# First norm's root multiplied in behind the u tiles' products, and three products of zeros on TensorE ahead of the first weights

## The chip, the cores and the metric

The kernel runs on one core of one Trainium2 chip. The core has five engines that run their own instruction streams and meet only at semaphores: TensorE (PE, matrix products into PSUM banks), VectorE (DVE), ScalarE (ACT), GpSimd (POOL) and SyncE (SP, which issues all of this kernel's transfers). The metric is device time in microseconds (us), as the median of several executions.

## The reference

A recurrent and attention block, and then two further blocks with their own mixers and feed-forwards, on 512 tokens of width 1024. Only its beginning matters here: the first norm, the projection to u and the convolution over u.

```python
D_MODEL = 1024
SEQ = 512
CONV_WIDTH = 4
def rms_norm(x, g):
    xf = x.astype(jnp.float32)
    y = xf * lax.rsqrt(jnp.mean(xf * xf, axis=-1, keepdims=True) + NORM_EPS)
    return (y * g.astype(jnp.float32)).astype(x.dtype)
...
        h = rms_norm(x, norm_g[l])
        proj = jnp.einsum("bsd,de->bse", h, w_in[l])
        u = proj[..., OFF_RNN_X:OFF_RNN_G]
...
        q = proj[..., OFF_Q:OFF_K].reshape(B, S, N_Q_HEADS, HEAD_DIM)
...
        u = causal_depthwise_conv(u, conv_w[l], conv_b[l])
        y_rnn = rg_lru(u, lru_w_a[l], lru_b_a[l], lru_w_x[l], lru_b_x[l], lru_lambda[l]) * jax.nn.silu(g_rnn)
```

The root is one number per token. The projection mixes features and not tokens, so the root can be multiplied in before the product or behind it; the gain g is one number per feature and must come before.

## The kernel before

Activations lie transposed: features on the 128 partitions in 8 chunks of 512 tokens each (`X`, `H_hi`, `H_lo`; `ch(t, k)` is chunk k). Every weight matrix is cut into tiles of 128 output features by 1024 input features, and the 269 tiles come in one stream in a fixed order: tiles 0 to 7 give u, 8 to 15 the queries (`T_Q` = 8), and so on. Products of 32-bit numbers are made as three faster ones: ACT rounds each half of a weight tile to `W_hi` (`split_hi`), DVE makes the rest `W_lo` (`split_lo`), and the activations are split in the same way, so that a tile costs 24 products of 128x512 (`linear`): W_hi by H_hi, W_hi by H_lo, W_lo by H_hi for each of 8 chunks. Tiles 0 and 1 are done together, chunk by chunk (`linear_pair`), because their chunks arrive one at a time from the norm.

The order of all work is written out by hand, engine by engine, with semaphores between. The start goes so: SP issues the parameters, four pairs of chunks of X, weight tile 0, the constants, weight tiles 1 to 3 and more, all in one queue. ACT squares the chunks, DVE adds the squares to `SS`, PE sums them over partitions (`square_sums`), DVE and ACT make the root (`variance`, `root`, `inverse`), PE spreads it over the partitions of a bank (`stat_rows`), and then DVE makes each chunk of X times gain times root (`norm_lo`, L1503), ACT its rounded part `H_hi` (L941), DVE its rest `H_lo` (L1495), and PE the pair.

Behind the pair, PE goes through tiles 2 to 7. After each it does the gates of a u tile that is ready (`gates(i)`, two products of 32-bit numbers). Meanwhile DVE goes through the u tiles in `U_ORDER` (L1543 to L1562): a step i waits for the tile's products, makes the convolution from the bank (one scaling, L1552, and three shifted multiply-adds, L1555, each waiting for the one before), frees the bank, then does one step of the later blocks' modulation (`ada_at`, L1447, from tile 2 on) and the rests of a coming weight tile (`split_lo(Tile(i + 1))`, for i above 2). PE starts tile t only when `lo_done` shows its W_lo. A short chain of 128x8 operations for the recurrence's constants (L1520 to L1531) stands on DVE ahead of the sums of squares. POOL writes zeros into three buffers at the start and later multiplies I by U (L1360).

Of the kernel before, what the change touches and what calls it, by code (L numbers as in the profile page):

```python
# [15 lines left out]
P = 128  # L16
S = 512
# [190 lines left out]
def build(nc, x, stream, ada, crow, lru_w, prm, cst, rope1, pos, out):  # L208
    with ExitStack() as ctx:
# [109 lines left out]
        stat_mm, t1_done, h_hi_done, h_lo_done = sem("stat_mm"), sem("t1_done"), sem("h_hi_done"), sem("h_lo_done")  # L319
        x_final = sem("x_final")  # L320
        u_done, gate_mm, gate_out = sem("u_done"), sem("gate_mm"), sem("gate_out")
        b2_done, root_b = sem("b2_done"), sem("root_b")
# [31 lines left out]
        def ch(t, j, n=S):  # L354
            return t[:, ds(j * S, n)]


        SPN = COL[:, 0:8]
# [26 lines left out]
        def _(sp):  # L385
# [14 lines left out]
            for k in range(4):  # L400
                sp.dma_start(X[:, 2 * k * S:2 * (k + 1) * S], x[:, 2 * k * S:2 * (k + 1) * S]).then_inc(x_in[k], 16)
            raw(Tile(0), False)
# [61 lines left out]
        def _(pe):  # L464
            def linear(tile, hi, lo, chunks=KC, first=None, between=None, own=True):

                dst = ps[tile.bank][:]
                free = tile.uses if own else tile.uses - 1
                if not (isinstance(free, int) and free == 0):
                    pe.wait_ge(bank_free[tile.bank], free)  # L470
                for half in range(2):
                    sl = (2 * tile.slot + half) % 4
                    pe.wait_ge(lo_done, tile.n * 2 + (half + 1))
                    ks = range(4 * half, min(4 * half + 4, chunks))
                    for k in ks:
# [4 lines left out]
                        pe.matmul(dst, wh, ch(hi, k), start=(k == 0), stop=False)  # L480
                        pe.matmul(dst, wh, ch(lo, k), start=False, stop=False)  # L481
                        mm = pe.matmul(dst, wl, ch(hi, k), start=False, stop=(k == chunks - 1))  # L482
# [28 lines left out]
            def linear_pair(t0, idx, bank=PAIR_BANK):  # L511
# [5 lines left out]
                for k in range(KC):  # L517
# [11 lines left out]
                    mm = pe.matmul(ps[b.bank][:], W_hi[:, at[1]:at[1] + P], ch(H_lo, k), start=False, stop=(k == 7))  # L529
                mm.then_inc(used, 2)  # L530

            def square_sums(z, parts, last, need=None):
# [119 lines left out]
            linear(Tile(T_Q), H_hi, H_lo, between=lambda k: gates(6 + k // 4) if k in (1, 5) else None)  # L652
            for c in range(1, 10):
# [257 lines left out]
        def _(act):  # L911
# [23 lines left out]
            def norm_hi(idx, shift=None, third=None):  # L935
                for k in range(KC):
                    if k == 7 and third is not None:
                        split_hi(third, (0,), ACT.Identity)
                    act.wait_ge(t1_done, 8 * idx + k + 1)
# [20 lines left out]
            act.activation(COL[:, 88:96], COL[:, 80:88], ACT.Exp).then_inc(prm_done, 1)  # L960
            for k in range(KC):
                if k % 2 == 0:
                    act.wait_ge(x_in[k // 2], 16)
                square(k, k)
            split_hi(Tile(0))
            split_hi(Tile(1))
# [8 lines left out]

            split_hi(Tile(2), (1,))
            act.wait_ge(crow_in, 16)
# [373 lines left out]
        def _(pool):  # L1351
# [67 lines left out]
        def _(dve):  # L1419
# [96 lines left out]
            dve.tensor_tensor(COL[:, 80:88], COL[:, 72:80], lam, ALU.min).then_inc(prm_done, 1)  # L1516

            dve.wait_ge(prm_done, 2)
            e = COL[:, 88:96]
# [12 lines left out]

            for k in range(KC - 2):
                sum_square(k, k == 0)
            dve.wait_ge(sq_done, 8)
            dve.tensor_tensor(ch(SQ, 1), ch(SQ, 0), ch(SQ, 1), ALU.add).then_inc(ss_step, 1)
            split_lo(Tile(0))
            split_lo(Tile(1))
            inv_rms(0)
            norm_lo(0, lambda k: pr("norm_g", k), None, Tile(2))  # L1540
            split_lo(Tile(2), (1,))

            for i, t in enumerate(U_ORDER):  # L1543
# [726 lines left out]
def STAT_ROWS(z):  # L2270

    return 2 * z + 2
# [88 lines left out]
```

## Time and profile before

| what | us |
|---|---|
| three runs | 1737.07, 1738.52, 1734.59; median 1737.07 |
| span of the profiled execution | 1734.7 |
| PE busy in it | 1668.1 (96%) |
| DVE, ACT, POOL busy | 1015.6 (59%), 703.0 (41%), 76.8 (4%) |
| first product of the pair begins | 19.23 |
| first product behind the pair (tile 2) begins | 31.97 |

The span runs from the first instruction of the core to its last; the profiled execution is one of its own, and no separate device time is shown for it beside the span. A busy share is a mean over 1.7 ms of stages; the change touches the first 80 us, and these are read from the rows by time.

### The profile page before, as it was taken

The page shows a single profiled execution, that of the slowest core. Times are in us where ns is not written, and L with a number is a line of the kernel's source. Part 1 is how long each engine was busy: PE and PEld are TensorE (multiplying, and loading weights), DVE is VectorE, ACT ScalarE, POOL GpSimd, SP SyncE. Part 2 cuts the span into 40 slices and gives each one's busy share as a digit, 9 for nine tenths or more (in the row PEclk, how much of TensorE's full clock was granted, in tenths as well). Part 3 has the DMA queues.
Part 4 walks back from the last instruction along what each step waited for, and adds up shares of the span by engine and source line. Part 5 has one row for each costly group of instructions (what it writes and reads, how often), then busy time and mean ns, then how long its engine had stood idle before and what let it go on. Part 6 is the DMA issues. An engine that isn't in the chain of part 4 may idle for free.

```text
span 1734.7 us, 23016 instructions
## 1 busy us (share of the span) xinstructions
PE 1668.1 (96%) x7756; PEld 1329.5 (77%) x7756; DVE 1015.6 (59%) x2004; ACT 703.0 (41%) x1329; POOL 76.8 (4%) x61
## 2 busy tenths in 40 slices
PE   6999999999999998888999999999999899999999
PEld 5777777778877775467888888887888788888887
DVE  7788876665467797835655563466454533333334
ACT  5364676653343335753333323234223433332322
POOL 0020000000000073100000000000000000000000
PEclk9999999999999998999999999999999999999999
DMA  6453444444331120002455553352333233333333
GB/s 241 158 158 113 146 153 154 156 149 137 97 97 49 49 86 25 1 25 73 170 193 194 193 195 121 121 182 86 97 97 97 73 98 97 97 97 97 97 97 110
DMA packets 56775, 202.82 MB, mean 117 GB/s; under 512 B 6576, under 2 KB 6704, under 8 KB 56560
## 3 DMA queue, kind: packets, MB, share of 16 engines
q1 hardware_dynamic: 56688, 201.68, 35.5%
q8 instruction: 52, 0.85, 0.2%
q14 instruction: 35, 0.29, 0.1%
HBM read 198.38 MB, written 2.10 MB: 116 GB/s over the span
## 4 chain that ended last, share of the span: by engine, by line
PE 88%; DVE 6%; ACT 2%; issue 2%; DMA 1%; SPq 0%; POOL 0%; DVEq 0%; ACTq 0%; POOLq 0%
PE bank L480 25%; PE bank L482 25%; PE bank L481 25%; PE bank L584 2%; PE bank L639 2%; PE bank L618 1%; PE bank L523 1%; PE bank L524 1%; DVE W_lo L1433 1%; PE bank L538 1%; DVE SB L2042 1%; DVE AW L1447 1%; PE bank L725 1%; PE bank L744 1%; PE bank L526 1%
## 5 line engine op out<-in xcount | busy, mean ns | idle before, releaser
L480 PE MATMUL bank<-H_hi,W_hi 128*128 128x512 f32 x1336 | 534.5, 400 | 3.3 <-DVE W_lo L1433 2.2
L481 PE MATMUL bank<-H_lo,W_hi 128*128 128x512 f32 x1336 | 521.7, 390 | 0.0
L482 PE MATMUL bank<-H_hi,W_lo 128*128 128x512 f32 x1336 | 521.6, 390 | 0.0
L1433 DVE TENSOR_TENSOR W_lo<-RAW,W_hi 128x512 fp32r<-128x512 f32 x538 | 351.4, 692 | 180.6 <-ACT W_hi L919 164.4
L919 ACT ACTIVATE W_hi<-RAW 128x512 fp32r<-128x512 f32 x538 | 317.3, 625 | 271.6 <-PE bank L482 235.3
L480 PEld LDWEIGHTS bank<-H_hi,W_hi 128*128 128x128 f32 x1336 | 251.3, 188 | 73.4 <-issue 19.7
L481 PEld LDWEIGHTS bank<-H_lo,W_hi 128*128 128x128 f32 x1336 | 251.6, 188 | 54.4 <-issue 4.5
L482 PEld LDWEIGHTS bank<-H_hi,W_lo 128*128 128x128 f32 x1336 | 251.4, 188 | 53.2
L482 PE MATMUL bank<-A_hi,W_lo 128*128 128x512 f32 x352 | 137.1, 390 | 0.0
L481 PE MATMUL bank<-A_lo,W_hi 128*128 128x512 f32 x352 | 137.1, 390 | 0.0
L480 PE MATMUL bank<-A_hi,W_hi 128*128 128x512 f32 x352 | 137.1, 389 | 0.0
L1447 DVE CUSTOM_DVE_ANT_0 AW<-AW,CROW 128x1024 f32<-128x1024 f32 x96 | 118.0, 1230 | 8.3 <-DVE X L2150 3.7
L1159 ACT ACTIVATE G<-bank 128x512 f32<-128x512 f32 x60 | 35.9, 598 | 170.3 <-PE bank L482 170.3
L956 ACT CAST A_hi<-Y 128x512 f32 (+1 forms) x44 | 27.3, 620 | 185.0 <-DVE Y L2122 185.0
L2122 DVE TENSOR_TENSOR Y<-bank,G 128x512 f32<-128x512 f32 x44 | 30.4, 692 | 118.0 <-PE bank L482 116.6
L480 PEld LDWEIGHTS bank<-A_hi,W_hi 128*128 128x128 f32 x352 | 66.1, 188 | 13.7
L482 PEld LDWEIGHTS bank<-A_hi,W_lo 128*128 128x128 f32 x352 | 66.1, 188 | 13.7
L481 PEld LDWEIGHTS bank<-A_lo,W_hi 128*128 128x128 f32 x352 | 66.1, 188 | 13.6
L2150 DVE SCALAR_TENSOR_TENSOR X<-bank,MOD,X 128x512 f32 x32 | 24.0, 751 | 75.9 <-PE bank L482 75.8
L2127 DVE TENSOR_TENSOR A_lo<-Y,A_hi 128x512 f32 (+1 forms) x44 | 30.5, 692 | 42.5 <-ACT A_hi L956 42.5
L584 PE MATMUL bank<-KD,Q 64*128 64x256 f32 (+3 forms) x256 | 45.8, 438 | 7.0 <-DVE SM L2042 3.1
L480 PE MATMUL bank<-YA_hi,W_hi 128*128 128x512 f32 x128 | 50.0, 391 | 1.6 <-DVE YA_lo L2084 1.6
(263 smaller groups left out, 2007.8 us busy)
## 6 DMA issues: line engine op xcount, KB each, us to landing
RAW<-weights SPq DMA_DIRECT2D x269, 512.0 KB, 3.7
AW<-ada SPq DMA_DIRECT2D x100, 512.0 KB, 3.7
X<-x_t SPq DMA_DIRECT2D x4, 512.0 KB, 5.5
y_t<-X SPq DMA_DIRECT2D x8, 256.0 KB, 2.0
LW<-lru_w SPq DMA_DIRECT2D x1, 1024.0 KB, 12.6
QX<-QR SPq DMA_DIRECT2D x40, 16.0 KB
CROW<-crow SPq DMA_DIRECT2D x1, 512.0 KB, 10.7
ROPE<-rope SPq DMA_DIRECT2D x1, 512.0 KB, 13.4
```

The lines of the kernel that those rows point to most:

```text
L480: pe.matmul(dst, wh, ch(hi, k), start=(k == 0), stop=False)
L481: pe.matmul(dst, wh, ch(lo, k), start=False, stop=False)
L482: mm = pe.matmul(dst, wl, ch(hi, k), start=False, stop=(k == chunks - 1))
L584: mm = pe.matmul(dst, Q[rows, chunk * S + n * P:chunk * S + (n + 1) * P], KD[rows, k0:k0 + w], start=True, stop=True)
L639: mm = pe.matmul(ps[6][odd * HD:(odd + 1) * HD, 0:2 * P], V[:, at_col:at_col + HD], PT[:, c * S + odd * 2 * P:c * S + (odd + 1) * 2 * P], ...
L919: act.activation(W_hi[:, sl * HALF:(sl + 1) * HALF], RAW[:, c:c + HALF], fn).then_inc(hi_done, 1)
L956: act.copy(dst, ch(Y2, par)).then_inc(a_hi_done, 1)
L1159: act.activation(ch(G1, par), ps[PAIR_BANK if first else ga.bank][:], fn).then_inc(fn_done, 1)
L1433: dve.tensor_tensor(W_lo[:, w], RAW[:, c:c + HALF], W_hi[:, w], ALU.subtract).then_inc(lo_done, 1)
L1447: dve.tensor_tensor_reduce(out=w, in0=w, in1=CROW[:], scale=1.0, scalar=0.0, op0=ALU.mult, op1=ALU.add, accum_out=MODQ[:, q:q + 1]).then_i ...
L2122: dve.tensor_tensor(ch(Y2, par), ps[tile.bank][:], ch(G1, par), ALU.mult).then_inc(prod_done, 1)
L2127: dve.tensor_tensor(ch(A_lo[g % 2], jj), ch(Y2, par), ch(A_hi[g % 2], jj), ALU.subtract).then_inc(a_lo_done, 1)
```

## The change

PE no longer waits for the root. The u tiles are made from X times gain (`XG_hi` from ACT, `XG_lo` from DVE), and DVE multiplies each u tile by the root when it takes it from the bank, into `G1`, from where the convolution now reads. The sums of squares go to PE between chunks 5 and 7 of the pair (`first_pair`), the spreading of the root into tile 2 (`first_rows`), and ACT copies it to `ROOT`. The true normed chunks are still needed from tile 8 on: POOL makes X times root (`XR`), and ACT and DVE split it (`x_true`) during tiles 2 to 6, by the table `TRUE_AT`. Two weight tiles are moved ahead of the last three pairs of X on SP, the chain of 128x8 operations moves behind the rests of tile 2 on DVE, and PE gets three products of zeros before the pair.

```diff
+        def xg_hi(k):
+            return ch(XG_hi, k)
...
+                if k == 0:
+                    raw(Tile(0), False)
+                    raw(Tile(1), False)
             sp.dma_start(CS[:], cst).then_inc(consts_in, 16)
-            for n in range(1, 4):
+            for n in range(2, 4):
...
+            def first_pair(a, b):
+
+                for k in range(KC):
+                    if k % 4 == 0:
+                        pe.wait_ge(lo_done, b.n * 2 + k // 4 + 1)
+                    pe.wait_ge(xg_hi_done, k + 1)
...
+                    pe.wait_ge(xg_lo_done, k + 1)
...
+                    if k == 5:
+                        pe.wait_ge(consts_in, 16)
+                        square_sums(0, (SS,), False, (ss_step, 6))
+                        square_sums(0, (ch(SQ, 1),), True, (ss_step, 7))
...
-            pe.wait_ge(consts_in, 16)
-            square_sums(0, (SS,), False, (ss_step, 6))
-            norm_stat(0, (ss_step, 7))
-            linear_pair(T_U, 0, 5)
+            def first_rows(k):
+                if k == 1:
+                    pe.wait_ge(rinv_done, 1)
+                    stat_rows(16, 2).then_inc(stat_mm, 1)
+
+            pe.wait_ge(pool_chain, 3)
+            for n in range(3):
+                pe.matmul(ps[3][:], QX1[0][:, 0:P], QX1[1][:, :], start=True, stop=True)
+            first_pair(Tile(T_U), Tile(T_U + 1))
             for t in range(T_U + 2, T_Q):
-                linear(Tile(t), H_hi, H_lo, own=t > 2)
+                linear(Tile(t), xg_hi, xg_lo, own=t > 2, between=first_rows if t == 2 else None)
                 gates(t - 2)
...
+            act.wait_ge(prm_in, 16)
+            for pair in range(4):
+                act.wait_ge(x_in[pair], 16)
+                x_gained(2 * pair)
+                x_gained(2 * pair + 1)
+                if pair == 0:
+                    split_hi(Tile(0))
+                    split_hi(Tile(1))
+                else:
+                    square(2 * pair - 2, 2 * pair - 2)
+                    square(2 * pair - 1, 2 * pair - 1)
...
             for t in range(T_U + 2, T_Q):
                 split_hi(Tile(t + 1))
+                for k in TRUE_AT[t]:
+                    x_true(k)
                 gates_out(t - 2)
...
+            pool.wait_ge(root_row, 1)
+            for k in range(KC):
+                pool.wait_ge(x_in[k // 2], 16)
+                if k >= 2:
+                    pool.wait_ge(h_lo_done, k - 1)
+                pool.tensor_tensor(ch(XR, k % 2), ch(X, k), ROOT[:, 0:S], ALU.mult).then_inc(xr_done, 1)
...
+            def x_true(k):
+                dve.wait_ge(h_hi_done, k + 1)
+                dve.scalar_tensor_tensor(out=ch(H_lo, k), in0=ch(XR, k % 2), scalar=pr("norm_g", k), in1=ch(H_hi, k),
+                                         op0=ALU.mult, op1=ALU.subtract).then_inc(h_lo_done, 1)
...
-                src = ps[5] if t == 0 else ps[tile.bank]
-
-                link(dve.tensor_scalar(ch(U, t), src[:], pr("conv_w", 24 + t), pr("conv_b", t), ALU.mult, ALU.add))
+                if i == 0:
+                    dve.wait_ge(root_row, 1)
+                src = ch(G1, i % 2)
+                link(dve.tensor_tensor(src, (ps[5] if t == 0 else ps[tile.bank])[:], ROOT[:, 0:S], ALU.mult))
+                dve.sem_inc(bank_free[tile.bank], 1)
+
+                link(dve.tensor_scalar(ch(U, t), src, pr("conv_w", 24 + t), pr("conv_b", t), ALU.mult, ALU.add))
...
                 dve.wait_ge(u_done, i + 1)
-                dve.sem_inc(bank_free[tile.bank], 1)
+                for k in TRUE_AT.get(i, ()):
+                    x_true(k)
                 ada_at(t)
...
+TRUE_AT = {2: (0, 1), 3: (2, 3), 4: (4,), 5: (5, 6), 6: (7,), 7: ()}
```

The order on the engines at the places that the prediction speaks of follows. First PE at the start of the program, before: the sums of squares (L538), the spread root (L545), then the pair (L523 on).

```order
L538 MATMUL bank4<-CS_88,SS_106 128x1 [waits ss_step,consts_in]
L538 MATMUL bank4<-CS_88,SS_106 128x1 x3
L538 MATMUL bank4<-CS_88,SQ_102 128x1 [waits ss_step]
L538 MATMUL bank4<-CS_88,SQ_102 128x1 x3
L545 MATMUL bank2<-CS_88,VC_109 128x128 [waits rinv_done]
```

And the same place in the changed kernel: the products of zeros (L690), then the pair's first chunk.

```order
L690 MATMUL bank<-QX_116,QX_115 128x512 [waits pool_chain]
L690 MATMUL bank<-QX_116,QX_115 128x512 x2
L556 MATMUL bank<-XG_hi,W_hi 128x512 [waits xg_hi_done,lo_done]
L557 MATMUL bank<-XG_hi,W_lo 128x512
L556 MATMUL bank<-XG_hi,W_hi 128x512
L557 MATMUL bank<-XG_hi,W_lo 128x512
L559 MATMUL bank<-XG_lo_122,W_hi 128x512 [waits xg_lo_done]
```

Nothing that waits for the root stands in front of the pair any more. Second, DVE in step i = 2 of the u tiles and up to step 3, before:

```order
L1552 TENSOR_SCALAR U<-bank,PR 128x512 [waits u_done,used]
L1555 SCALAR_TENSOR_TENSOR U<-bank,PR,U 128x511 [waits dve_chain]
L1555 SCALAR_TENSOR_TENSOR U<-bank,PR,U 128x510 [waits dve_chain]
L1555 SCALAR_TENSOR_TENSOR U<-bank,PR,U 128x509 [waits dve_chain]
L1447 ISA AW,MODQ<-AW,CROW 128x1024 [waits u_done,crow_done,ada_in0]
```

and the same step in the changed kernel (V is the memory that `ROOT` takes, G_113 is `G1`):

```order
L1637 TENSOR_TENSOR G_113<-bank,V 128x512 [waits used,u_done]
L1640 TENSOR_SCALAR U<-G_113,PR 128x512 [waits dve_chain]
L1643 SCALAR_TENSOR_TENSOR U<-G_113,PR,U 128x511 [waits dve_chain]
L1643 SCALAR_TENSOR_TENSOR U<-G_113,PR,U 128x510 [waits dve_chain]
L1643 SCALAR_TENSOR_TENSOR U<-G_113,PR,U 128x509 [waits dve_chain]
L1593 SCALAR_TENSOR_TENSOR H_lo<-XR,PR,H_hi 128x512 [waits h_hi_done,u_done]
L1593 SCALAR_TENSOR_TENSOR H_lo<-XR,PR,H_hi 128x512 [waits h_hi_done]
L1515 ISA AW,MODQ<-AW,CROW 128x1024 [waits crow_done,ada_in0]
L1515 ISA MODQ 128x1
L1501 TENSOR_TENSOR W_lo<-RAW,W_hi 128x512 [waits hi_done] x2
```

The step has one instruction more in front, two rests of true chunks behind the convolution, and its shifted multiply-adds read two SBUF buffers where they read a bank and one buffer. Third, POOL in the changed kernel, behind its zeros; of these rows only the last was there before.

```order
L1424 TENSOR_TENSOR XR<-X,V 128x512 [waits x_in0,root_row,pool_chain]
L1424 TENSOR_TENSOR XR<-X,V 128x512 [waits x_in0]
L1424 TENSOR_TENSOR XR<-X,V 128x512 [waits h_lo_done,x_in1] x2
L1424 TENSOR_TENSOR XR<-X,V 128x512 [waits h_lo_done,x_in2] x2
L1424 TENSOR_TENSOR XR<-X,V 128x512 [waits h_lo_done,x_in3] x2
L1428 TENSOR_TENSOR I<-I,U 128x512 [waits u_done,gate_out] x8
```

Eight products of two SBUF buffers now run on POOL during the u tiles; from the third on each waits for a rest that DVE has made.

## Rows read from the trace of the kernel before

**Rows 1.** The page, parts 1 and 4: busy time, and the chain by engine.

```profile
PE 1668.1 (96%) x7756; PEld 1329.5 (77%) x7756; DVE 1015.6 (59%) x2004; ACT 703.0 (41%) x1329; POOL 76.8 (4%) x61
PE 88%; DVE 6%; ACT 2%; issue 2%; DMA 1%; SPq 0%; POOL 0%; DVEq 0%; ACTq 0%; POOLq 0%
```

**Rows 2.** Timeline 0 to 40 us: start, duration, instruction, idle time before it.

```profile
3.41 0.17 DVE L1520 TENSOR_SCALAR COL<-COL 128x8 f32<-128x8 f32 x1 [0.27 <-ACT COL L960]
...
5.34 1.15 ACT L928 ACTIVATE SQ<-X 128x512 f32<-128x512 f32 x2 [1.96 <-DMA X<-x_t]
...
6.55 0.17 DVE L1531 TENSOR_SCALAR COL<-COL 128x8 f32<-128x8 f32 x1
...
11.54 1.87 PE L538 MATMUL bank<-CS,SS 128*128 128x1 f32 x8 [11.54 <-DMA CS<-constants]
...
19.23 0.77 PE L523 MATMUL bank<-H_hi,W_hi 128*128 128x512 f32 x1 [1.58 <-ACT H_hi L941]
...
21.50 0.63 PE L529 MATMUL bank<-H_lo,W_hi 128*128 128x512 f32 x1
...
21.93 0.63 PE L523 MATMUL bank<-H_hi,W_hi 128*128 128x512 f32 x1
...
28.34 0.39 PE L523 MATMUL bank<-H_hi,W_hi 128*128 128x512 f32 x1
...
28.57 0.39 PE L524 MATMUL bank<-H_hi,W_lo 128*128 128x512 f32 x1
...
31.97 0.39 PE L480 MATMUL bank<-H_hi,W_hi 128*128 128x512 f32 x1
```

**Rows 3.** The page, part 6: transfers, size, time from issue to landing.

```profile
CROW<-crow SPq DMA_DIRECT2D x1, 512.0 KB, 10.7
ROPE<-rope SPq DMA_DIRECT2D x1, 512.0 KB, 13.4
```

**Rows 4.** Timeline of SP 0 to 140 us: the issues of these two.

```profile
5.87 0.58 SPq L406 DMA_DIRECT2D CROW<-crow  x1
...
6.97 0.49 SPq L408 DMA_DIRECT2D ROPE<-rope  x1
```

**Rows 5.** Timeline of DVE in the u tiles.

```profile
33.27 0.81 DVE L1552 TENSOR_SCALAR U<-bank,PR 128x512 f32<-128x512 f32 x1
...
59.46 0.81 DVE L1552 TENSOR_SCALAR U<-bank,PR 128x512 f32<-128x512 f32 x1 [1.07 <-PE bank L482]
...
66.66 0.81 DVE L1552 TENSOR_SCALAR U<-bank,PR 128x512 f32<-128x512 f32 x1 [1.22 <-PE bank L482]
...
71.24 1.29 DVE L1433 TENSOR_TENSOR W_lo<-RAW,W_hi 128x512 fp32r<-128x512 f32 x2
```

**Rows 6.** Timeline of PE at the start of tile 8 (after gates 5).

```profile
75.62 0.40 PE L481 MATMUL bank<-H_lo,W_hi 128*128 128x512 f32 x1
...
76.97 0.30 PEld L564 LDWEIGHTS bank<-U,LW 128*128 128x128 f32 x2 [0.46 <-issue]
```

**Rows 7.** Timeline of POOL.

```profile
84.86 12.37 POOL L1360 TENSOR_TENSOR I<-I,U 128x512 f32<-128x512 f32 x8 [82.65 <-ACT I L974]
```

**Rows 8.** Timeline of DVE, beside POOL's products and behind them.

```profile
92.08 1.78 DVE L1567 SCALAR_TENSOR_TENSOR T<-G,T 128x512 f32<-128x512 f32 x1
...
100.53 0.69 DVE L1567 SCALAR_TENSOR_TENSOR T<-G,T 128x512 f32<-128x512 f32 x1 [0.15 <-DVE Q L1586]
```

**Rows 9.** DVE's groups by line and form: busy, mean ns of one, idle before.

```profile
L2122 DVE TENSOR_TENSOR Y<-bank,G 128x512 f32<-128x512 f32 x44 | 30.4, 692 | 118.0 <-PE bank L482 116.6 <-ACT G L1159 1.3
...
L1497 DVE SCALAR_TENSOR_TENSOR H_lo<-G,MOD,H_hi 128x512 fp32r<-128x512 f32 x32 | 23.9, 748 | 1.0
```

**Rows 10.** Line 2196, a scaling from SBUF to SBUF: ns min/median/max.

```profile
L2196 DVE TENSOR_SCALAR ZC<-Y,PR x8: 481/486/488, 1202.5 to 1276.7; 128x512 f32 x6, 128x512 f32<-128x512 f32 x2
```

**Rows 11.** Busy time by stretch, with PE's granted clock (the number before the DMA share).

```profile
520.00:530.00 10.00, 7.51 (x25) 6.04 (x26) 7.90 (x16) 3.76 (x6) 0.00 (x0) 0.59 0.00 1
```

More of the change, by code:

```diff
@@ L256, in build @@
         W_lo = at("W_lo", 4 * HALF, dt=F32R)
+        kd = cursor[0]
         KD = at("KD", NKV * S)
@@ L355, in ch, with xg_lo @@
             return t[:, ds(j * S, n)]
+        def xg_hi(k):
+            return ch(XG_hi, k)
+        def xg_lo(k):
+            return ch(XG_lo[0], k) if k < 4 else ch(XG_lo[k // 2 - 1], k % 2)
         SPN = COL[:, 0:8]
@@ L479, in linear @@
                         wh, wl = W_hi[:, c:c + P], W_lo[:, c:c + P]
-                        pe.matmul(dst, wh, ch(hi, k), start=(k == 0), stop=False)
-                        pe.matmul(dst, wh, ch(lo, k), start=False, stop=False)
-                        mm = pe.matmul(dst, wl, ch(hi, k), start=False, stop=(k == chunks - 1))
+                        hk, lk = (hi(k), lo(k)) if callable(hi) else (ch(hi, k), ch(lo, k))
+                        pe.matmul(dst, wh, hk, start=(k == 0), stop=False)
+                        pe.matmul(dst, wh, lk, start=False, stop=False)
+                        mm = pe.matmul(dst, wl, hk, start=False, stop=(k == chunks - 1))
                         if k == ks[-1]:
@@ L530, in linear_pair @@
                 mm.then_inc(used, 2)
+            def first_pair(a, b):
[3 more added lines that the diff above has]
+                    pe.wait_ge(xg_hi_done, k + 1)
+                    at = [((2 * tile.slot + k // 4) % 4) * HALF + (k % 4) * P for tile in (a, b)]
+                    for dst, c in zip((ps[5], ps[b.bank]), at):
+                        pe.matmul(dst[:], W_hi[:, c:c + P], xg_hi(k), start=(k == 0), stop=False)
+                        pe.matmul(dst[:], W_lo[:, c:c + P], xg_hi(k), start=False, stop=False)
+                    pe.wait_ge(xg_lo_done, k + 1)
+                    mm = pe.matmul(ps[5][:], W_hi[:, at[0]:at[0] + P], xg_lo(k), start=False, stop=(k == 7))
+                    if k % 4 == 3:
+                        mm.then_inc(used, 1)
+                    mm = pe.matmul(ps[b.bank][:], W_hi[:, at[1]:at[1] + P], xg_lo(k), start=False, stop=(k == 7))
+                    if k == 7:
+                        mm.then_inc(used, 2)
+                    if k == 5:
+                        pe.wait_ge(consts_in, 16)
+                        square_sums(0, (SS,), False, (ss_step, 6))
+                        square_sums(0, (ch(SQ, 1),), True, (ss_step, 7))
             def square_sums(z, parts, last, need=None):
@@ L960, in _, with x_gained @@
             act.activation(COL[:, 88:96], COL[:, 80:88], ACT.Exp).then_inc(prm_done, 1)
[L961 to L966, printed above, removed]
+            def x_gained(k):
+                act.activation(xg_hi(k), ch(X, k), ACT.Identity, scale=pr("norm_g", k)).then_inc(xg_hi_done, 1)
+            def x_true(k):
+                act.wait_ge(xr_done, k + 1)
+                act.activation(ch(H_hi, k), ch(XR, k % 2), ACT.Identity, scale=pr("norm_g", k)).then_inc(h_hi_done, 1)
+            act.wait_ge(prm_in, 16)
[9 more added lines that the diff above has]
+                    square(2 * pair - 1, 2 * pair - 1)
+            square(6, 6)
+            square(7, 7)
             root(0, 1)
-            norm_hi(0, None, Tile(2))
+            split_hi(Tile(2), (0,))
             def gates_out(i):
@@ L976, in _ @@
             split_hi(Tile(2), (1,))
+            act.wait_ge(stat_mm, STAT_ROWS(0))
+            act.copy(ROOT[:, 0:S], ps[2][:]).then_inc(root_row, 1)
             act.wait_ge(crow_in, 16)
@@ L1516, in _, with x_rest, x_true @@
             dve.tensor_tensor(COL[:, 80:88], COL[:, 72:80], lam, ALU.min).then_inc(prm_done, 1)
+            def x_rest(k):
+                dve.wait_ge(xg_hi_done, k + 1)
+                dve.scalar_tensor_tensor(out=xg_lo(k), in0=ch(X, k), scalar=pr("norm_g", k), in1=xg_hi(k),
+                                         op0=ALU.mult, op1=ALU.subtract).then_inc(xg_lo_done, 1)
+            def x_true(k):
+                dve.wait_ge(h_hi_done, k + 1)
+                dve.scalar_tensor_tensor(out=ch(H_lo, k), in0=ch(XR, k % 2), scalar=pr("norm_g", k), in1=ch(H_hi, k),
+                                         op0=ALU.mult, op1=ALU.subtract).then_inc(h_lo_done, 1)
+            for pair in range(4):
+                dve.wait_ge(x_in[pair], 16)
+                x_rest(2 * pair)
+                x_rest(2 * pair + 1)
+                if pair == 0:
+                    split_lo(Tile(0))
+                    split_lo(Tile(1))
+                else:
+                    sum_square(2 * pair - 2, pair == 1)
+                    sum_square(2 * pair - 1, False)
+            dve.wait_ge(sq_done, 8)
+            dve.tensor_tensor(ch(SQ, 1), ch(SQ, 0), ch(SQ, 1), ALU.add).then_inc(ss_step, 1)
+            variance(0, 1)
+            inverse(0, 1)
+            split_lo(Tile(2))
             dve.wait_ge(prm_done, 2)
@@ L1531, in _ @@
             dve.tensor_scalar(COL[:, 72:80], acc, -1.0, None, ALU.mult).then_inc(prm_done, 2)
[L1533 to L1541, printed above, removed]
             for i, t in enumerate(U_ORDER):
```

12 lines of the change are left out of this document (9 added, 3 removed).

## The prediction

> **What bounds the kernel now.** I read the page first. PE is busy 96% of the span and makes up 88% of the chain that ended last [rows 1]; so what the first 80 us gain or lose stays, unless a later engine takes it up, and a time saved is one by which PE's stream moves forward. Then the timeline of the start. PE idles until 19.23 because its pair needs normed chunks, and these need all squares, their sums over partitions (the first four sums begin at 11.54) and the root [rows 2]. The pair ends where tile 2 begins, at 31.97. Its early products follow each other in 0.43 (21.50 to 21.93), later ones in 0.23 (28.34 to 28.57) [rows 2]: half and full pace. Behind the pair the question is which engine ends each tile. On DVE the first two waits for PE that I find in the u tiles are 1.07 at 59.46 and 1.22 at 66.66 [rows 5]; ahead of them it goes from one step to the next. So before the change PE sets the pace only from about tile 5 on, and DVE has about 1 us a tile to spare. That is the narrow place that the change loads.
>
> **The early start.** The queue lands 512 KB every 1.27 us: CROW lands at 5.87 + 10.7 = 16.6, ROPE at 6.97 + 13.4 = 20.4, with 1.5 MB of the two transfers up to ROPE in those 3.8 us [rows 3, 4]. The first pair of X is there at 5.3 [rows 2], so in the new order weight tiles 0 and 1 land at 6.6 and 7.9 and the last pair of X at 11.7. PE needs three halves of W_lo; ACT's third rounding ends near 8.5 and DVE's rest near 9.2. The pair begins at 9.3 and not at 19.23. It has 48 products of 0.23 = 10.9, and the sums between take two blocks like the 1.87 of the row [rows 2], at half of that if the clock is high: 1.9 in all. That ends at 22.1; the first products at half pace add up to 1.6, and the last squares, which ACT and DVE make by turns among the splits, hold the second block back by some tenths. I take 23.5. The pair ends 31.97 - 23.5 = 8.5 earlier.
>
> If nothing else stood in the way, PE would go on as before: 43.4 us from there to the first product of tile 8 (75.4, one product ahead of the row at 75.62 [rows 6]), and 1 for spreading the root inside tile 2 (estimate: half of the two blocks of sums). That is 67.9 and a gain of 7.5.
>
> **What DVE is given instead.** I follow DVE from the pair's end to the rests of weight tile 8.
> - The second half of tile 2 must wait for the pair's last product, as before: 33.27 - 31.97 = 1.3 [rows 2, 5]. DVE is free at 24.8.
> - The chain of 128x8 operations, once under the wait for X, takes 6.72 - 3.41 = 3.3 [rows 2] with nothing over it now: 28.1.
> - The work of before from the first scaling to the rests of tile 8 is 71.24 - 33.27, less the waits of 1.07 and 1.22: 35.7 [rows 5]. 63.8.
> - Seven products with the root are ahead of that place. One is like 2122's product of a bank and an SBUF buffer, 0.69 [rows 9], and 0.03 for the wait on it. The scaling behind it now reads SBUF: 0.49 [rows 10] where the bank took 0.81 [rows 5]. Net 0.40 each, 2.8: 66.6. The bank comes free earlier, which nobody waits for.
> - Eight rests of true chunks are like line 1497, 0.75 [rows 9], 0.68 where the next need not wait (the two of 1.29 at 71.24 [rows 5] overlap by some 0.08): 5.4. 72.0. Before, norming and its rests were work under PE's wait; now six rests of X times gain lie there, and the true ones lie here.
> - POOL's eight products. POOL took 12.37 for eight of that size [rows 7], 1.55 each, and beside it a DVE instruction with two SBUF inputs took 1.78, against 0.69 behind it [rows 8]: 1.09 lost for each POOL product that meets one. Products three to eight are released by DVE's own rests, in the middle of its busy stretch, and what follows there has two SBUF inputs (rest, modulation, split). Nothing is lost where the product with the root or a wait is next; the most is 8 times 1.55 = 12.4. I take six meetings of 1.09 = 6.5, since all six releases lie between such instructions: 78.5.
>
> The first half of tile 8's rests ends 0.69 later, at 79.2, and the second product of tile 8 begins near 79.5; before it was 75.62 [rows 6]. The 3.9 shrink a little, because PE no longer idles 0.46 ahead of gates 6 [rows 6]. **The sum is +3.6.** ACT gets 16 roundings more and 8 less, but idles in the u tiles; its x_true waits for POOL stand ahead of `gates_out`, and behind those PE's next gates, a whole tile later. SP's queue lands the same bytes, and weight tile 4 is wanted after 40. The three products of zeros end before 9.3 and cost PE nothing.
>
> The Trainium skill speaks to the sixth item (SBUF — State Buffer, "Who interferes with whom"): a DVE instruction with two SBUF inputs and a GpSimd instruction that reads SBUF exclude each other for the whole instruction, and "Issue order, not op shape, decides who blocks." By that last sentence DVE, always first here, could lose nothing, and the sum would be the -2.9 of the first rival. The rows above show turns instead, both sides slowed.
>
> **Its own time.** The profiled execution spans 1734.7, at the low end of the three runs; the same shift on the median 1737.07 gives 1740.7. A difference under 0.2% (3.5 us) can hardly be told from none in this kernel.
>
> **Rivals.**
> 1. POOL's products hide beside DVE's bank reads or wait for DVE. Then 6.5 falls away: 3.6 - 6.5 = -2.9, 1734.2. For it: the convolution's first product still reads a bank. Against it: rows 8, and the releases lie ahead of the modulation. It decides where a meeting costs under 0.6 us (3.6 / 6). Chance 0.17.
> 2. DVE is not in the way at all and PE's lead stays: -7.5, 1729.6. It would need the 18 us of added work to vanish under PE's; against it stand only two waits of about 1 us. Chance 0.05.
> 3. TensorE's clock falls in the pair. Between 520 and 530, where a later norm makes PE wait in the same way, the granted clock was 0.59 [rows 11]. If the clock stands at its lower level for the last two chunks behind the sums, 12 products take 0.23 more each, 2.7, all of it on DVE's path, since the half weight tile waits for the pair: +6.3, 1743.4. For it: the sums are thin work. Against it: PE's pause there is tenths of a us. Later falls, in tile 4 where PE waits some 4 us for W_lo, are hidden by DVE. Chance 0.18.
>
> The forecast has 0.60, with its own bounds of about 3 either way (four to eight meetings, the pair's end 0.5 earlier or 1 later): 1737.5 to 1743.5.
>
> **How the numbers follow.** The range runs from just above the first rival to past the third: 1734.0 to 1745.5. Below it lie the second rival and half of the first; above it a case with low clock and more meetings. Slower by over 0.2% means above 1740.5: a little over half of the forecast (0.31) and nearly all of the third (0.17), 0.48. Faster means below 1733.6: the second rival and some 0.06 of the first, 0.11. The rest, 0.41, is no change that can be told.
>
> **What would show it.** The pair's first product near 9.3 and tile 2 near 23.5 show the early start. Most of PE's lead should go in one place, a wait of 4 to 5 us for W_lo ahead of tile 4 (there the rests of tile 4 stand behind DVE's first two true rests and two of POOL's products), and the remainder in waits of 1 to 3 us at tiles 5 and 7. DVE should have no wait on PE in the u tiles. Six DVE instructions between 40 and 70 should take over 1.6 where their kind takes 0.7 to 1.2. The second product of tile 8 near 79.5 shows the sum; from there on the distance between the traces should stay. I am wrong if DVE waits for PE in these tiles, if the instructions beside POOL keep their time, or if tile 8 begins before 75.6.

## The result, and the profile after

The changed kernel takes 1745.77 us (median of four runs, 1742.65 to 1747.74), the kernel before on the same chip 1737.80 (1734.59 to 1739.19): a ratio of 1.0050, interval 1.0037 to 1.0062. It is 0.5% slower, about 8 us; the forecast was +3.6, and the time lies 0.3 above the range.

The profiled execution spans 1740.9 where the one before spanned 1734.7. The page, part 4, against the second of [rows 1]:

```profile
PE 86%; DVE 9%; ACT 2%; issue 2%; POOL 0%; DMA 0%; SPq 0%; DVEq 0%; ACTq 0%; POOLq 0%
```

PE's share of the chain fell from 88 to 86%, DVE's rose from 6 to 9%. So look at the start. PE's timeline, as in [rows 2, 6]: start, duration, instruction, and in brackets the idle time before it with what ended it.

```profile
1.79 4.59 PE L690 MATMUL bank<-QX,QX 128*128 128x512 f32 x6 [1.79 <-POOL QX L1416]
9.39 0.79 PE L556 MATMUL bank<-XG_hi,W_hi 128*128 128x512 f32 x1 [3.00 <-DVE W_lo L1501]
...
25.13 0.39 PE L496 MATMUL bank<-XG_hi,W_hi 128*128 128x512 f32 x1
...
35.70 1.74 PE L602 MATMUL bank<-U,LW 128*128 128x512 f32 x2 [4.49 <-DVE U L1643]
...
49.90 0.76 PE L496 MATMUL bank<-XG_hi,W_hi 128*128 128x512 f32 x1 [3.34 <-DVE W_lo L1501]
...
59.55 0.47 PE L496 MATMUL bank<-XG_hi,W_hi 128*128 128x512 f32 x1 [0.68 <-DVE W_lo L1501]
...
67.44 0.47 PE L496 MATMUL bank<-XG_hi,W_hi 128*128 128x512 f32 x1 [0.46 <-DVE W_lo L1501]
...
76.18 0.47 PE L496 MATMUL bank<-XG_hi,W_hi 128*128 128x512 f32 x1 [1.32 <-DVE W_lo L1501]
...
83.67 0.40 PE L497 MATMUL bank<-H_lo,W_hi 128*128 128x512 f32 x1
```

The pair's first product begins at 9.39, 9.84 earlier than before. Tile 2 begins at 25.13, 6.84 earlier. The second product of tile 8 begins at 83.67, 8.05 later than the 75.62 of [rows 6], so 14.9 us go between the two. Five waits, each of them ended by DVE, make 10.3 of it: 4.49 ahead of the first gates, 3.34 ahead of tile 4, and 0.68, 0.46 and 1.32 ahead of tiles 5, 6 and 7. Most of the rest is half pace behind the first two of them (the gates from 35.70, and products 0.43 apart from 50.47 to 53.03) and the spreading of the root in tile 2. Ahead of tile 8 PE has no wait: it comes there from the gates behind tile 7.

DVE's timeline, as in [rows 2, 5]:

```profile
26.44 0.16 DVE L1614 TENSOR_SCALAR COL<-COL 128x8 f32<-128x8 f32 x1
...
27.48 3.79 DVE L1621 SCALAR_TENSOR_TENSOR COL<-COL 128x8 f32<-128x8 f32 x8
...
31.89 0.69 DVE L1637 TENSOR_TENSOR G<-bank,V 128x512 f32<-128x512 f32 x1
...
45.77 2.32 DVE L1515 CUSTOM_DVE_ANT_0 AW<-AW,CROW 128x1024 f32<-128x1024 f32 x1
...
48.02 2.34 DVE L1501 TENSOR_TENSOR W_lo<-RAW,W_hi 128x512 fp32r<-128x512 f32 x2
...
64.37 1.22 DVE L1515 CUSTOM_DVE_ANT_0 AW<-AW,CROW 128x1024 f32<-128x1024 f32 x1
...
82.15 1.29 DVE L1501 TENSOR_TENSOR W_lo<-RAW,W_hi 128x512 fp32r<-128x512 f32 x2
```

And POOL's:

```profile
27.85 2.59 POOL L1424 TENSOR_TENSOR XR<-X,V 128x512 f32<-128x512 f32 x2 [25.65 <-ACT V L1036]
45.34 3.88 POOL L1424 TENSOR_TENSOR XR<-X,V 128x512 f32<-128x512 f32 x2 [14.89 <-DVE H_lo L1593]
54.94 3.92 POOL L1424 TENSOR_TENSOR XR<-X,V 128x512 f32<-128x512 f32 x2 [5.73 <-DVE H_lo L1593]
```

The chain of 128x8 operations begins at 26.44 and the first product with the root at 31.89, 5.45 later; the eight operations of L1621 take 3.79 of that, and POOL's first two products (27.85 to 30.44) lie over them. At 45.77 a modulation step takes 2.32, at 64.37, without POOL, the same takes 1.22; at 48.02 two rests take 2.34, where [rows 5] have 1.29. POOL's second pair lies over those. DVE has no wait for PE in the u tiles.

The 8.05 of tile 8 answer to the 8.0 between the medians. The two spans differ by 6.2 only. The profiled execution of the changed kernel is the fastest of its four, and with the two traces laid side by side, instruction by instruction, the distance can be followed: 7.5 us at the first product of queries by keys (159.35 against 151.82), 9.1 to 9.3 from 181 to 675 us, then 5.6 from 700 us and 4.0 from 735 to 815. Where it falls, the granted clock of the kernel before was 0.57 from 670 to 680 and 0.84 from 680 to 690, that of the changed one 0.83 and 1.00 in the same work (679 to 689 and 689 to 699). The change touches nothing there, so I go by the medians.

### The profile page after: what moved, and what is told of

It is laid out like the page before. It is cut to its first block, busy times and chain, and to the rows that moved or that the text cites. A ratio compares the mean times of both kernels' runs of the same rounds, so it can differ in the third digit from the quotient of the medians.

```text
span 1740.9 us, 23072 instructions
## 1 busy us (share of the span) xinstructions
PE 1671.9 (96%) x7762; PEld 1330.1 (76%) x7762; DVE 1026.7 (59%) x2012; ACT 707.9 (41%) x1338; POOL 90.9 (5%) x69
## 4 chain that ended last, share of the span: by engine, by line
PE 86%; DVE 9%; ACT 2%; issue 2%; POOL 0%; DMA 0%; SPq 0%; DVEq 0%; ACTq 0%; POOLq 0%
PE bank L496 25%; PE bank L498 24%; PE bank L497 24%; PE bank L622 2%; PE bank L677 2%; DVE W_lo L1501 1%; PE bank L656 1%; PE bank L539 1%; DVE AW L1515 1%; PE bank L540 1%; DVE U L1643 1%; PE bank L576 1%; PE bank L769 1%; PE bank L788 1%; DVE SB L2131 1%
## 5 line engine op out<-in xcount | busy, mean ns | idle before, releaser
L496 PE MATMUL bank<-H_hi,W_hi 128*128 128x512 f32 x1288 | 513.9, 399 | 3.1 <-DVE W_lo L1501 2.1
L497 PE MATMUL bank<-H_lo,W_hi 128*128 128x512 f32 x1288 | 503.0, 391 | 0.0
L498 PE MATMUL bank<-H_hi,W_lo 128*128 128x512 f32 x1288 | 503.0, 391 | 0.0
L496 PEld LDWEIGHTS bank<-H_hi,W_hi 128*128 128x128 f32 x1288 | 242.4, 188 | 69.7 <-issue 17.4
L497 PEld LDWEIGHTS bank<-H_lo,W_hi 128*128 128x128 f32 x1288 | 242.4, 188 | 51.6 <-issue 3.6
L498 PEld LDWEIGHTS bank<-H_hi,W_lo 128*128 128x128 f32 x1288 | 242.3, 188 | 51.1
```

Of the source, the lines that this page charges most:

```text
L496: pe.matmul(dst, wh, hk, start=(k == 0), stop=False)
L497: pe.matmul(dst, wh, lk, start=False, stop=False)
L498: mm = pe.matmul(dst, wl, hk, start=False, stop=(k == chunks - 1))
```

## Experiments

Theory A: POOL's products take turns with DVE's instructions, and the DVE path through the u tiles ends PE's tiles. Theory B: DVE's path is long by the number of its added operations, and POOL is harmless. Theory C: TensorE's clock in the pair makes the loss. Ratios are to the kernel before on the same chip. e1 to e4, e5 to e8 and e9 with e10 each shared a chip, with 1738.66, 1736.97 and 1737.58 for the kernel before, so runs are compared by the ratios. The changed kernel's own ratio rests on four runs, and a difference of 0.2% between two ratios is weak by itself; the rows of the traces go with it.

| run | us | ratio to before | interval |
|---|---|---|---|
| changed kernel | 1745.77 | 1.0050 | 1.0037 to 1.0062 |
| e1_no_pool | 1737.98 | 0.9993 | 0.9984 to 1.0002 |
| e2_chain_first | 1742.97 | 1.0030 | 1.0018 to 1.0042 |
| e3_no_zeros | 1744.14 | 1.0031 | 1.0021 to 1.0040 |
| e4_six_zeros | 1743.70 | 1.0038 | 1.0026 to 1.0050 |
| e5_dve_root | 1740.89 | 1.0020 | 1.0011 to 1.0029 |
| e6_pool_twice | 1753.79 | 1.0090 | 1.0072 to 1.0108 |
| e7_all | 1732.76 | 0.9977 | 0.9967 to 0.9986 |
| e8_before_ada | 1736.24 | 0.9992 | 0.9982 to 1.0002 |
| e9_after_ada | 1740.35 | 1.0024 | 1.0015 to 1.0034 |
| e10_all_no_zeros | 1732.44 | 0.9978 | 0.9967 to 0.9990 |

### POOL's products left out

```diff
-                pool.tensor_tensor(ch(XR, k % 2), ch(X, k), ROOT[:, 0:S], ALU.mult).then_inc(xr_done, 1)
...
-                act.activation(ch(H_hi, k), ch(XR, k % 2), ACT.Identity, scale=pr("norm_g", k)).then_inc(h_hi_done, 1)
+                act.activation(ch(H_hi, k), ch(X, k), ACT.Identity, scale=pr("norm_g", k)).then_inc(h_hi_done, 1)
```

> POOL's eight products of X by the root are left out, and the true chunks are split from X itself, so the root is missing in them; ACT and DVE issue the same instructions as in the changed kernel. Theory A (turns between POOL and DVE make the loss): the chain of 128x8 operations takes 3.3 again instead of 5.45, the six long DVE instructions between 45 and 73 go back to 1.2 to 1.4, and the rests of tile 8 begin near 73.3 instead of 82.15; the time falls by 8 to 9 us, to about 2 us under the kernel before. Theory B (the instructions added on DVE make it, POOL only shifts the wait): the rests of tile 8 begin above 79 and the time falls by less than 3. Theory C (TensorE's clock in the pair): no more than 2 us change.

The whole loss is gone: 0.9993. The root is missing in the true chunks of this run; its times alone are of use. DVE's timeline, then PE's:

```profile
25.84 0.17 DVE L1607 TENSOR_SCALAR COL<-COL 128x8 f32<-128x8 f32 x1
...
26.88 1.57 DVE L1614 SCALAR_TENSOR_TENSOR COL<-COL 128x8 f32<-128x8 f32 x8
...
29.07 0.69 DVE L1630 TENSOR_TENSOR G<-bank,V 128x512 f32<-128x512 f32 x1
...
72.77 1.29 DVE L1494 TENSOR_TENSOR W_lo<-RAW,W_hi 128x512 fp32r<-128x512 f32 x2
```

```profile
32.87 1.12 PE L602 MATMUL bank<-U,LW 128*128 128x512 f32 x2 [2.28 <-DVE U L1636]
...
44.92 0.47 PE L496 MATMUL bank<-XG_hi,W_hi 128*128 128x512 f32 x1 [2.86 <-DVE W_lo L1494]
...
75.66 0.40 PE L497 MATMUL bank<-H_lo,W_hi 128*128 128x512 f32 x1
```

The eight operations of the chain are back at 1.57, the chain at 29.07 - 25.84 = 3.23, and the rests of tile 8 begin at 72.77 where they began at 82.15. Of these 9.4, DVE's earlier start is 0.6, the chain 2.2, and the six instructions beside POOL's other products 6.6. The number of DVE's instructions is the same in both kernels, so B can't make this difference. PE shows why no POOL is no gain either: it waits 2.28 for the first convolution and 2.86 ahead of tile 4, its next products follow at half pace (46.28 to 48.84), and from there it has no wait up to tile 8, whose second product begins at 75.66: the 75.62 of [rows 6] again.

### The chain moved to the front of DVE

The 16 instructions of the chain go from behind `split_lo(Tile(2))` to the place ahead of the loop over the pairs of X.

> The chain of 128x8 operations stands again where it stood before, ahead of DVE's first rests. Theory A: its 5.45 behind tile 2 go away, but its first end is near 6.7, so the first rests and the pair come about 1 us later, and POOL's first two products now meet the first convolution and the rests of tile 3 instead; the rests of tile 8 begin 1 to 3 us earlier than 82.15, and the time falls by 1 to 3 us. Theory B (the chain itself is the lost cover): the full 5.4 come back less about 1, rests of tile 8 near 77.5, time 4 to 5 us lower.

```profile
27.26 0.69 DVE L1637 TENSOR_TENSOR G<-bank,V 128x512 f32<-128x512 f32 x1 [1.29 <-ACT V L1036]
28.11 0.79 DVE L1640 TENSOR_SCALAR U<-G,PR 128x512 f32<-128x512 f32 x1 [0.16 <-DVE G L1637]
28.93 3.26 DVE L1643 SCALAR_TENSOR_TENSOR U<-G,PR,U 128x511 f32<-128x511 f32 x3
...
78.72 1.29 DVE L1501 TENSOR_TENSOR W_lo<-RAW,W_hi 128x512 fp32r<-128x512 f32 x2
```

The first product with the root begins at 27.26 and not at 31.89. It waits for the root's copy in SBUF now (1.29). POOL's first two products (27.30 to 30.08 in this trace) lie over a scaling and three shifted multiply-adds, which take 0.79 and 3.26 for 0.55 and 2.32: 1.2 lost and not 2.2. The rests of tile 8 begin at 78.72, 3.4 earlier than in the changed kernel, of which 0.55 is an earlier end of the pair (24.58). That is past the 1 to 3 of A and short of the 77.5 of B, and it is the rows that show the place of the chain to be part of the loss. The time can't: it is 0.2% below the changed kernel by the ratios, but so is that of e3 below, whose rests of tile 8 are no earlier (83.22).

### No zeros, and six

```diff
-            for n in range(3):
+            for n in range(6):
```

> The three products of zeros are left out. Theory C (the clock in the pair costs 1.6): if the zeros help, the pair's slow products grow from 14 and the pair ends later than 25.1, by up to 1.5; if, as I think, the pause of 3 us behind the zeros undoes them, the pair has the same or fewer slow products (8 in the kernel before) and ends within 0.5 of 25.1. The time is the same within 1.5 us either way, as DVE's rests and squares run beside it.

> Six products of zeros instead of three, so that they end near 9 and no pause is left ahead of the pair. Theory C: the pair runs at full pace from its first product, ends near 23.2 instead of 25.1, and the rests of tile 8 begin 1.5 to 2 us earlier; the time falls by 1.5 to 2 us. Rival: DVE and ACT hold the pair's chunks back anyway, and the pair ends no more than 0.5 us earlier.

PE's timeline without zeros:

```profile
10.63 0.76 PE L556 MATMUL bank<-XG_hi,W_hi 128*128 128x512 f32 x1 [10.63 <-DVE W_lo L1499]
...
26.19 0.39 PE L496 MATMUL bank<-XG_hi,W_hi 128*128 128x512 f32 x1
```

and with six products of zeros, then one of its stretches:

```profile
10.55 0.50 PE L556 MATMUL bank<-XG_hi,W_hi 128*128 128x512 f32 x1 [0.49 <-DVE W_lo L1501]
...
19.33 1.02 PE L576 MATMUL bank<-CS,SS 128*128 128x1 f32 x8 [0.32 <-DVE SS L1532]
20.63 1.36 PE L576 MATMUL bank<-CS,SQ 128*128 128x1 f32 x8 [0.27 <-DVE SQ L1607]
...
22.42 0.63 PE L557 MATMUL bank<-XG_hi,W_lo 128*128 128x512 f32 x1
22.85 0.63 PE L556 MATMUL bank<-XG_hi,W_hi 128*128 128x512 f32 x1
...
25.98 0.40 PE L496 MATMUL bank<-XG_hi,W_hi 128*128 128x512 f32 x1
```

```profile
20.50:23.00 2.50, 2.37 (x11) 2.18 (x12) 0.59 (x5) 1.31 (x3) 0.00 (x0) 0.65 1.01 405
```

From its first product to tile 2 the pair lasts 26.19 - 10.63 = 15.6 without zeros, 25.13 - 9.39 = 15.7 with three, and 25.98 - 10.55 = 15.4 with six. With three, PE idles 3.00 behind the zeros and the granted clock, 0.97 from 5 to 9 us, is 0.50 in the next two stretches, of which this is the first, and 0.90 from 15 to 18 (busy time of PE, PEld, DVE, ACT, POOL, then the granted clock):

```profile
9.00:12.00 3.00, 2.61 (x6) 2.13 (x7) 2.77 (x6) 2.89 (x6) 0.00 (x0) 0.50 1.03 415
```

0.50 is the lower level (1.2 GHz), and the first 14 products follow each other in 0.43. With six there is no such pause, and products go at full pace from the first one. But then PE gets to the sums early, waits for the squares (0.32 and 0.27), is thinly busy in the sums themselves, and the clock falls behind them: 0.65 in that stretch, products at 0.43 from 21.85 to 24.55. That is the mechanism of the prediction's third rival. The half pace moves from one end of the pair to the other. The pair ends at 25.98, not at the 23.2 expected of theory C, and neither kernel is told from the changed one by its time. One trace of each is not much, though: in the seven traces of this record with three zeros the pair lasts 14.3 to 14.5 five times and 15.6 or 15.7 twice, in the two without zeros 15.6 and 14.8. What sets the length in one execution stays open. Theory C has a part in the pair's end (below), and no run shows the zeros to be worth more than about 1 us.

### The products on DVE, and POOL's products doubled

```diff
+            def x_root(i):
+                for k in TRUE_AT.get(i, ()):
+                    if k >= 2:
+                        dve.wait_ge(h_lo_done, k - 1)
+                    dve.tensor_tensor(ch(XR, k % 2), ch(X, k), ROOT[:, 0:S], ALU.mult).then_inc(xr_done, 1)
...
                 ada_at(t)
+                x_root(i + 1)
```

POOL's loop over these products goes.

> The changed kernel with the eight products X times root made by DVE itself, one step of the u tiles ahead of their rests; POOL makes none. Theory A (a POOL product beside DVE's instructions costs DVE about 1.1 us, more than the product would cost DVE itself): leaving POOL's products out brought the rests of weight tile 8 from 82.2 to 72.8; eight products of 0.61 to 0.69 put 5.2 back, so 78.0, and the time is 4 below the changed kernel, 1741.7 (1740 to 1743). Theory B (it is the number of operations on the path of the u tiles, wherever they are made): DVE gets eight instructions more and the time is the changed kernel's 1745.8 or above it. The chain of 128x8 operations should take its 3.3 again by A.

```profile
37.50 1.29 DVE L1589 TENSOR_TENSOR XR<-X,V 128x512 f32<-128x512 f32 x2
...
77.27 1.29 DVE L1495 TENSOR_TENSOR W_lo<-RAW,W_hi 128x512 fp32r<-128x512 f32 x2
```

The rests of tile 8 begin at 77.27 (78.0 expected), 4.9 earlier than in the changed kernel, of which 0.9 is DVE's earlier start; the time is 0.3% below the changed kernel by the ratios. A DVE that does POOL's work itself is faster than one that has it done: a pair of such products takes DVE 1.29 here, and POOL's pair cost it 2.2.

```diff
+                pool.tensor_tensor(ch(XR, k % 2), ch(X, k), ROOT[:, 0:S], ALU.mult).then_inc(pool_chain, 1)
+                pool.wait_ge(pool_chain, 4 + k)
                 pool.tensor_tensor(ch(XR, k % 2), ch(X, k), ROOT[:, 0:S], ALU.mult).then_inc(xr_done, 1)
```

> The changed kernel with each of POOL's eight products made twice, the same values into the same buffer. Theory A: each further product that lies beside DVE's two-input instructions costs 1.1, eight of them 7 to 9: the rests of weight tile 8 at 89.5 to 91 and the time near 1753. Theory B: DVE has no instruction more, POOL is idle for most of the u tiles, so the time stays at 1745.8 within 1.

It came nearly as A says: 1753.79, and the rests of tile 8 at 89.34, with not one instruction more on DVE. The two timelines side by side show how the turns go, DVE first:

```profile
28.15 5.75 DVE L1623 SCALAR_TENSOR_TENSOR COL<-COL 128x8 f32<-128x8 f32 x8
...
47.07 1.41 DVE L1595 SCALAR_TENSOR_TENSOR H_lo<-XR,PR,H_hi 128x512 fp32r<-128x512 f32 x2
48.40 2.32 DVE L1517 CUSTOM_DVE_ANT_0 AW<-AW,CROW 128x1024 f32<-128x1024 f32 x1
...
50.66 3.46 DVE L1503 TENSOR_TENSOR W_lo<-RAW,W_hi 128x512 fp32r<-128x512 f32 x2
54.03 0.68 DVE L1639 TENSOR_TENSOR G<-bank,V 128x512 f32<-128x512 f32 x1
...
81.53 1.10 DVE L1521 COPY MODR<-MODQ 128x4 f32<-128x4 f32 x1
...
89.34 1.29 DVE L1503 TENSOR_TENSOR W_lo<-RAW,W_hi 128x512 fp32r<-128x512 f32 x2
```

```profile
47.96 1.67 POOL L1424 TENSOR_TENSOR XR<-X,V 128x512 f32<-128x512 f32 x1 [14.09 <-DVE H_lo L1595]
49.72 2.13 POOL L1426 TENSOR_TENSOR XR<-X,V 128x512 f32<-128x512 f32 x1
...
53.64 1.65 POOL L1426 TENSOR_TENSOR XR<-X,V 128x512 f32<-128x512 f32 x1
```

POOL's product issued at 47.96 takes 1.67: it waits for the end of the rest that DVE is in (to 48.5) and then runs some 1.2. The modulation step that DVE issues at 48.40 waits for POOL to end at 49.63 and takes 1.1 more (1.22 alone). The next product of POOL, issued at 49.72, waits for that. In these rows whoever waits gets the next turn, and a product of POOL holds up the one instruction of DVE that is issued behind it, unless that reads a bank. The extra cost can be added up: 5.75 - 3.79 in the chain, three pairs of rests 1.1 longer each, 0.9 on the small copy at 81.53 (0.17 in the changed kernel), 0.3 on two scalings: 6.5, and 0.7 from a later start, 7.2. So six of the eight further products cost 0.9 to 1.1 each, and the two that meet a product with the root and the scaling behind it 0.16 each. The rests of tile 8 begin at 89.34 where they began at 82.15.

### All four edits, and its control

```diff
+ADA_TWO = range(T_FILL + 8, T_FILL + 17, 1)
+ADA_TILES = sorted([*range(11, T_V - 2), *range(T_FILL, T_MA + 4), *ADA_TWO])
...
-                elif i > 2:
-                    split_lo(Tile(i + 1))
...
                 dve.wait_ge(u_done, i + 1)
+                if 2 <= i < T_Q - 1:
+                    split_lo(Tile(i + 2))
                 for k in TRUE_AT.get(i, ()):
                     x_true(k)
```

With these, the chain at the front and the products on DVE, as above.

> Four edits to the changed kernel: DVE makes the products X times root itself; the chain of 128x8 operations stands first on DVE again; the rests of the next weight tile stand ahead of the true rests and the modulation step; and nine modulation steps (those of tiles 2 to 10) move into nine tiles of the stage behind 200 us, where PE was busy all the time and DVE had slack, two steps in one tile there. If DVE alone took the early start away, then about 11 us come out of its path up to tile 8 and about 2 in the query tiles: tile 8 begins near 73 where it was 75.4 before the change, the time is 1734 (1732 to 1737), 3 to 4 below the kernel before. If something else holds PE back (weight transfers, ACT's roundings, the gates), tile 8 begins at 75 or later and the time is 1738 or above.

> The kernel before the change, with only the nine modulation steps moved as in the run with four edits. It is the control for that run: what the move gives without the early start. The waits of PE for DVE's rests there were 0.46, 0.34 and 1.66, so 2 to 2.5 us: 1736 (1735 to 1738). If it gives as much as the run with all four edits, the early start is worth nothing even with DVE unloaded; if it gives 2 and the other 4 or more, the early start is worth the difference.

PE's timeline with all four edits:

```profile
10.12 0.55 PE L558 MATMUL bank<-XG_hi,W_hi 128*128 128x512 f32 x1 [2.91 <-DVE W_lo L1497]
...
31.07 1.13 PE L604 MATMUL bank<-U,LW 128*128 128x512 f32 x2 [0.43 <-DVE U L1643]
...
40.81 1.72 PE L604 MATMUL bank<-U,LW 128*128 128x512 f32 x2 [2.27 <-ACT I L1034]
...
73.34 0.40 PE L499 MATMUL bank<-H_lo,W_hi 128*128 128x512 f32 x1
```

Two waits are left, 0.43 for the first convolution and 2.27 for ACT's second gate output, and the second product of tile 8 begins at 73.34, 2.3 before that of [rows 6]. The time is 0.9977 of the kernel before (0.9967 to 0.9986), so this version is faster than both. The control, the moved steps alone, gives 0.9992: 0.7 us by the medians, short of the 2 to 2.5 expected and with an interval that reaches 1. Its trace has the 2.5, between tile 8 (77.01 against 75.62) and the first product of queries by keys (150.72 against 151.82); half of it is lost again near 243, where two steps stand in one tile. The control lacks the third edit, the earlier rests, but its PE has no wait between the pair and 92 us that these could take away. The rest, 1736.24 - 1732.76 = 3.5 (2.6 by the two ratios), is what the early start is worth once DVE can follow. The traces agree: at the first product of queries by keys the run with four edits (146.45) is 4.3 ahead of the control, and 1.0 of that is a pair that began late in the control's execution (20.20 against 19.23).

### The moved steps alone in the changed kernel; all four edits without zeros

> The changed kernel with only the nine modulation steps moved into the stage behind 200 us; POOL's products and the place of the chain are as in the change. If DVE's path through the u tiles sets the end, six steps of 1.22 leave it (some of the meetings with POOL then fall on the rests of weight tiles instead): the rests of weight tile 8 begin near 75.5 where they began at 82.2, tile 8 begins near 77, and with the 2 of the query tiles the time is 7 to 8 below the changed kernel, 1738 (1736.5 to 1740). If POOL sets the end (its products late, so that the true rests wait), DVE would only wait longer for POOL and the time would fall by less than 3.

```profile
45.09 3.50 DVE L1503 TENSOR_TENSOR W_lo<-RAW,W_hi 128x512 fp32r<-128x512 f32 x2
...
75.63 1.29 DVE L1503 TENSOR_TENSOR W_lo<-RAW,W_hi 128x512 fp32r<-128x512 f32 x2
```

The path came out as expected: rests of tile 8 at 75.63. With the step gone, both of POOL's products fall on the two rests of a weight tile, 3.50 for 1.29: the meetings stay, 1.1 each, and only the steps' own time leaves. The time, 1740.35, is 0.35 above the expected range, and by the ratios it is 4.5 below the changed kernel where I had 7 to 8. The 2 us of the query tiles are in the trace: the second product of tile 8 begins at 78.28, 2.7 behind the kernel before, the first product of queries by keys at 151.54, 0.3 ahead of it. They go later. 1.25 is lost where two steps stand in one tile (PE gets waits of 0.35 and 0.52 near 244, where there were none, as in the control's trace), and 1.5 between 381 and 512, where the granted clock was 0.91 from 380 to 400 and 1.00 in the kernel before. The first belongs to the edit; whether the second does is open.

> The kernel with all four edits, without the three products of zeros in front of the pair. The rows so far show the pair lasting 15.7 with three products of zeros, 15.6 without, 15.4 with six, so the zeros should be worth nothing: the time of the run with all four edits, 1732.8, within 1.5. If the zeros help where DVE no longer hides the pair's end, the pair ends 1 to 1.5 later and the time is 1734 or above.

1732.44 at a ratio of 0.9978, against 0.9977 with the zeros: the time shows nothing of them there either. In the two traces the pair ends 0.6 later without them (25.19 against 24.58), and the second product of tile 8 begins 0.6 later (73.95 against 73.34).

## Why the prediction was wrong

The direction and the mechanism were right, the sum was under half of what came. Two terms made it so: the chain of 128x8 operations, where I had overlooked POOL's first two products (2.2), and the end of the pair, which was sized too early (1.6). By the prediction's own steps:

- **The pair begins at 9.3**: 9.39.
- **It ends at 23.5**: 25.13. My terms, 22.1 and 1.6 and some tenths, already gave about 24, and I took 23.5. The term "the first products at half pace add up to 1.6" was for eight products. There were 14, at 0.2 each 2.8. In the trace before the clock had risen within eight products of the pair; here it stood at 0.50 behind PE's 3.00 of pause, and e1, with the same zeros, had it only from 11.3 to 14.7 (pair's end 24.53). This term varies from run to run by some 1 us, and the profiled execution has the longest pair of the seven with three zeros; in the five where it lasts 14.3 to 14.5 it ends at 24.2 to 24.6. It cost 1.6 here, a size that was off and not a mechanism.
- **The chain takes 3.3 "with nothing over it now"**: 5.45. This is the step whose mechanism failed: an overlap that I put at nothing. I had POOL's products three to eight meet DVE, because those are released between DVE's instructions, and gave the first two to the time in which DVE would be elsewhere. They begin when the root is in SBUF, 27.85, and that is inside the chain. It cost 2.2, and e1 (3.23) and e2 show it.
- **Seven products with the root 2.8, eight true rests 5.4, six meetings of 1.09**: from the first product with the root to the rests of tile 8 the sum had 78.5 - 28.1 = 50.4; measured 82.15 - 31.89 = 50.3. The six meetings are there, 1.05 to 1.12 each, and without POOL it is 72.77 - 29.07 = 43.7, where the sum had 43.9. That is in part luck: a product with the root and the wait on it take 0.85 and not 0.72, and the waits of 0.15 to 0.27 that DVE had behind each convolution before the change are gone.
- **The second product of tile 8 at 79.5**: 83.67, later by the 1.6 and 2.2 above and by 0.5 (it begins 1.5 behind the start of the rests, where I had 1.0), less 0.1. The 0.5 is PE's own: its last wait is ahead of tile 7, and it is still in the gates when the rests are ready. The 0.46 ahead of gates 6, which was to shrink the distance by 0.3, is there in the changed kernel too (84.59 to 85.05).
- **The waits**: I had 4 to 5 us ahead of tile 4 and the remainder at tiles 5 and 7. Ahead of tile 4 it was 3.34. The largest, 4.49, is ahead of the first gates, since the late chain holds up the first convolution; I had not followed DVE's delay to the gates at all.

The rivals: **POOL hidden** (-2.9) fell, and its price was wrong besides. Without POOL the time equals the one before, since PE has lost its lead in two waits and a stretch of half pace before DVE's ledger counts; a sum on DVE alone was no time for that case. **PE's lead stays** fell. **The clock falls behind the sums** did not happen in the changed kernel, where PE had no wait ahead of them; it did with six zeros. Its price was 12 times 0.23, where the rows give 0.43 - 0.23 = 0.20, so 2.4 and not 2.7.

The Trainium skill (SBUF — State Buffer, "Who interferes with whom") had the exclusion for the whole instruction, and the trace agrees: in e6 the product with the root, one input in a bank, takes 0.68 at 54.03 with POOL at work, and the instructions with two SBUF inputs wait. I read its "Issue order, not op shape, decides who blocks." as a case in which DVE loses nothing. The rows bear the sentence out in another sense: POOL's issue at 47.96 is ahead of DVE's at 48.40, and DVE blocks.

## What to carry to other kernels

Work handed to POOL is not free for a busy DVE: here DVE paid 1.1 us for each POOL product that it could have made itself in 0.65. It depends on the instruction beside it: a product with one input in a bank kept its 0.68, a scaling of one SBUF buffer lost 0.16 to 0.24, and a copy of a small one 0.9, nearly as much as the instructions with two SBUF inputs. Before a transfer or a product is called "early", follow its release to the very instruction that it lands on, small ones too: eight operations on 128x8 numbers lost as much as one pair of large ones. And a lead on PE is worth only what the engine that feeds it can follow: the same early start cost 8 us with DVE full, and gave about 3 once DVE had been unloaded.

## What the runs showed of the hardware

Operations with two SBUF inputs of 128x8 numbers, 0.2 each, were held up by POOL as large ones were: eight of them took 1.57 alone, 3.79 beside two products of POOL, 5.75 beside four, so 1.0 to 1.1 for each product. A copy of 128x4 numbers took 1.10 beside POOL and 0.17 without. And the column of the granted clock does not show every slow stretch: without zeros it stands at 1.00 over the whole pair, though products follow each other in 0.43 from 11.19 to 16.31; the spacing of products is the surer reading.
